# A two-block network on one core: low parts of one weight on GpSimd, rope angles and modulation part 2 in other places

## What is computed

```
mod = c @ w_ada[l] + b_ada[l]
shift_m, scale_m, gate_m, shift_f, scale_f, gate_f = jnp.split(mod, 6, axis=-1)
h = modulate(rms_norm(x, g_pre_mix[l]), shift_m, scale_m)
proj = h @ w_in[l]
q_a, k_a, v_a, q_m, k_m, v_m, o_m, i_m, f_m, g_a, g_m = jnp.split(proj, split_points, axis=-1)
q_a, k_a = rope(q_a, positions), rope(k_a, positions)        # sliding-window attention
qk_m = silu(causal_depthwise_conv(concat([q_m, k_m])))       # mLSTM in chunks of 64
merged = sigmoid(g_a) * (y_a @ w_branch_attn) + sigmoid(g_m) * (y_m @ w_branch_mlstm)
x = x + gate_m * rms_norm(merged @ w_out, g_post_mix)
h2 = modulate(rms_norm(x, g_pre_ffn), shift_f, scale_f)
x = x + gate_f * rms_norm((silu(h2 @ w_gate) * (h2 @ w_up)) @ w_down, g_post_ffn)
```

## Time and profile before

| | |
|---|---|
| median of 3 runs | 820.08 us (815.45 to 822.45) |
| the profiled execution | 822.01 us, of which its span is 820.2 us |
| PE busy | 767.2 us, 94% of the span |
| DVE busy | 638.1 us, 78% |
| ACT busy | 393.8 us, 48% |
| POOL busy | 29.0 us, 4% |
| DMA | 173.67 MB, mean 212 GB/s |

### The profile page before, as it was taken

One profiled execution on the slowest core, in us unless ns is written; L12 is line 12 of the kernel. 1 busy time (PEld: TensorE's weight loads), 2 busy tenths in 40 slices (PEclk: granted clock), 3 DMA queues, 4 the chain that ended last, 5 costly groups with the idle time before them and its releaser, 6 DMA issues.

```text
span 820.2 us, 15828 instructions
## 1 busy us (share of the span) xinstructions
PE 767.2 (94%) x6598; PEld 702.9 (86%) x6598; DVE 638.1 (78%) x838; ACT 393.8 (48%) x554; POOL 29.0 (4%) x44
## 2 busy tenths in 40 slices
PE   0999998998998999999999999989998999999996
PEld 0888998997887999999878987889878999999874
DVE  5759988888986887867987899886599678556457
ACT  3356753575464445344354894533125544454440
POOL 0110000000001000000001000050010000000000
PEclk9999999999999999999999999999999999999999
DMA  9795586682656999989992643600363679565621
GB/s 357 255 343 200 163 258 230 208 281 83 218 188 191 343 318 309 321 279 318 345 348 86 222 147 116 200 3 3 105 226 109 207 243 340 177 196 190 196 97 52
DMA packets 96021, 173.67 MB, mean 212 GB/s; under 512 B 7768, under 2 KB 55231, under 8 KB 95951
## 3 DMA queue, kind: packets, MB, share of 16 engines
q1 hardware_dynamic: 93630, 166.62, 60.9%
q0 software_dynamic: 1872, 5.86, 2.4%
q10 hardware_dynamic: 448, 0.19, 0.1%
HBM read 171.60 MB, written 1.05 MB: 210 GB/s over the span
## 4 chain that ended last, share of the span: by engine, by line
PE 69%; DVE 18%; DMA 6%; ACT 4%; issue 3%; DVEq 0%; POOL 0%; ACTq 0%; POOLq 0%
PE bank L2087 12%; PE bank L2088 12%; PE bank L2089 12%; PE bank L2352 5%; PE bank L2354 4%; PE bank L2353 4%; DVE wlo L459 3%; PE bank L2062 2%; PE bank L2064 2%; PE bank L2063 2%; DMA raw<-in_w_in 2%; DMA cc<-in_c 2%; PE bank L2514 1%; DVE acc L486 1%; DMA raw<-in_w_ada 1%
## 5 line engine op out<-in xcount | busy, mean ns | idle before, releaser
L650 ACT ACTIVATE whi<-raw 128x1024 fp32r<-128x1024 f32 (+1 forms) x212 | 220.9, 1053 | 225.4 <-PE bank L2089 99.2
L459 DVE TENSOR_TENSOR wlo<-raw,whi 128x1024 fp32r<-128x1024 f32 (+1 forms) x212 | 254.2, 1214 | 87.0 <-ACT whi L650 83.3
L2087 PE MATMUL bank<-hh,whi 128*128 128x256 f32 x1016 | 286.3, 282 | 10.7 <-DVE wlo L459 7.4
L2088 PE MATMUL bank<-hl,whi 128*128 128x256 f32 x1016 | 283.8, 279 | 0.0
L2089 PE MATMUL bank<-hh,wlo 128*128 128x256 f32 x1016 | 283.7, 279 | 0.0
L2087 PEld LDWEIGHTS bank<-hh,whi 128*128 128x128 f32 x1016 | 193.1, 190 | 14.8 <-issue 10.2
L2088 PEld LDWEIGHTS bank<-hl,whi 128*128 128x128 f32 x1016 | 192.6, 190 | 0.4 <-issue 0.2
L2089 PEld LDWEIGHTS bank<-hh,wlo 128*128 128x128 f32 x1016 | 192.5, 189 | 0.0
L486 DVE SCALAR_TENSOR_TENSOR acc<-raw,cc,acc 128x1024 f32<-128x1024 f32 x56 | 71.7, 1280 | 5.5 <-DMA raw<-in_w_ada 3.3
L2352 PE MATMUL bank<-whi,ffh 128*128 128x512 f32 x168 | 65.6, 391 | 0.9 <-DVE wlo L459 0.9
L2353 PE MATMUL bank<-wlo,ffh 128*128 128x512 f32 x168 | 65.4, 389 | 0.0
(11 more groups left out here) (453 smaller groups left out, 1081.2 us busy)
## 6 DMA issues: line engine op xcount, KB each, us to landing
raw<-in_w_ada SPq DMA_DIRECT2D x96, 512.0 KB, 5.2
raw<-in_w_in SPq DMA_DIRECT2D x54, 512.0 KB, 4.6
raw<-in_w_ffn_in SPq DMA_DIRECT2D x88, 256.0 KB, 3.9
raw<-in_w_ffn_gate SPq DMA_DIRECT2D x44, 256.0 KB, 4.3
...
```

The source lines that it names most:

```text
L459: eng.tensor_tensor(lo[:, 0:nk * width], raw[:, b % RAW, 0:nk * width], hi[:, 0:nk * width].bitcast(fp), ALU.subtract)\
L650: act.activation(weight_place(g)[0][:, 0:nk * width], raw[:, b % RAW, 0:nk * width], ACT.Copy)\
L2087: mm(o, wh[:, k, c], xh[:, kk_, :], start=first, stop=False)
L2088: mm(o, wh[:, k, c], xl[:, kk_, :], start=False, stop=False)
```

## The change

In the order of the program:

1. The low parts of blocks 2 to 5 of `o_if` are made on POOL, not on DVE. ACT makes the high parts of blocks 4 and 5 between the halves of its scaling, not behind it. POOL does this ahead of its first broadcast loads, and four of these loads now wait until ACT has copied the first half of `qm` (`conv_raw`).
2. PE runs 52 fillers before it turns x, and 40 where it had 32.
3. The angles move behind `km` on DVE, and the biases and `osig` ahead of or into `km`. ACT's sine moves behind its copy of `qm`, ahead of its high parts of `vm`. The small transfers are issued three before each block from number 33 on.
4. Part 2 (`c4`, `c5`) lies beside `km` and `vm`. `kva` and `g1` have nothing beside them; `c6`, `c7`, `c8` lie beside `g2`, `g3`, `ba0`. PE sums part 2 behind `g1`, with 8 fillers in its middle and 8 behind it; the transposes of k that follow wait for DVE to have taken it.

```diff
@@ -110,8 +110,8 @@
-    head = ["c0", "c1", "c2", "c3", "o_if", "qm", "km", "vm", "g0", "qa", "kva", "c8", "g1", "c4", "g2", "c5",
-            "g3", "c6", "ba0", "c7", "ba1", "bm0", "bm1", "wo0", "c9", "wo1"]
+    head = ["c0", "c1", "c2", "c3", "o_if", "qm", "km", "c4", "vm", "c5", "g0", "qa", "kva", "g1", "g2", "c6",
+            "g3", "c7", "ba0", "c8", "ba1", "bm0", "bm1", "wo0", "c9", "wo1"]
     first = [x for j in range(FT // 2) for x in ([f"ff{j}"] + ([f"c{BESIDE_FF[j]}"] if j in BESIDE_FF else []))]
     middle = ["lora", "k", "r", "v", "pv", "pu", "wo2a", "wo3a", "c21", "wo2b", "wo3b"]
@@ -403,7 +403,11 @@
-        ready = [("dve", b + 1) for b in range(len(order))]
+        ready, made_by = [], {"dve": 0, "pool": 0}
+        for o in order:
+            who = "pool" if o[0] == "o_if" and 2 <= o[1] < 6 else "dve"
+            made_by[who] += 1
+            ready.append((who, made_by[who]))
         of_split = {o[6]: b for b, o in enumerate(order) if o[6] is not None}
@@ -421,7 +425,7 @@
         def part_place(d):
-            return {0: (0, 0), 1: (1, 0), 2: (2, 0), 3: (2 * (place["wo0"][0] % 2), 0), 4: (6, 0), 5: (4, 0), 6: (4, 6), 7: (4, 7),
+            return {0: (0, 0), 1: (1, 0), 2: (5, 0), 3: (2 * (place["wo0"][0] % 2), 0), 4: (6, 0), 5: (4, 0), 6: (4, 6), 7: (4, 7),
                     8: (5, 0), 9: (5, 0), 10: (6, 0), 11: (4, 0)}[d]
@@ -529,8 +533,8 @@
                     sp.wait_ge(sem(f"{who}_blocks"), count)
-                if 28 <= b < 37:
-                    for n in (2 * (b - 28), 2 * (b - 28) + 1):
+                if 33 <= b < 39:
+                    for n in range(3 * (b - 33), 3 * (b - 33) + 3):
                         small_transfer(n)
                     sp.dma_start(cut(raw, b % RAW, nk, width)[:, :, a:z], src).then_inc(sem(f"raw{b % RAW}_in"), 16)
@@ -552,6 +556,8 @@
+            prepare_on(pool, "pool", "o_if")
+
@@ -572,6 +578,7 @@
             pool.wait_ge(sem("spreads"), 3 * 16)
+            pool.wait_ge(sem("conv_raw"), 1)
             spread(bcs[:, 1, :], A["sg_ln_g_2"][0], sem("spreads"))
             spread(bc[:, 0, :], A["g_post_mix"][0], sem("spreads"))
@@ -650,7 +657,7 @@
-            def scale_h(u):
+            def scale_h(u, between=None):
                 sh = modT[:, u // 2, (24 if u % 2 else 0):(32 if u % 2 else 8)]
@@ -668,6 +675,8 @@
                            .then_inc(sem("hh_ready"), 1)
+                    if between and half == 0:
+                        between()
@@ -691,8 +700,8 @@
             split("o_if", slice(0, 4))
-            scale_h(0)
-            split("o_if", slice(4, 8))
+            scale_h(0, lambda: split("o_if", slice(4, 6)))
+            split("o_if", slice(6, 8))
             split("qm")
             b0, b1 = item("o_if")
@@ -702,9 +711,6 @@
-
-            act.wait_ge(sem("angles"), 1)
-            act.activation(cossin, rsc[:, 1], ACT.Sin).then_inc(sem("cossin_ready"), 1)
                 for h, b in enumerate(item(name)):
@@ -716,6 +722,8 @@
                 if nxt:
+                    act.wait_ge(sem("angles"), 1)
+                    act.activation(cossin, rsc[:, 1], ACT.Sin).then_inc(sem("cossin_ready"), 1)
                     split(nxt)
             act.wait_ge(sem("if_turned"), 1)
@@ -1194,6 +1202,17 @@
+            dve.wait_ge(sem("osig_ready"), 1)
+            dve.wait_ge(sem("spreads"), 3 * 16)
+            for m in range(MT):
+                TT(st[:, 240 + 8 * m:248 + 8 * m], bank[4 + m][:, 252:260], bsm[:, 0:8], ALU.add)\
+                    .then_inc(sem("if_ready"), 1)
+
+            prepare("km", slice(0, 1))
+            dve.wait_ge(sem(f"pair{place['o_if'][0] % 2}_free"), place["o_if"][0] // 2 + 1)
+            for m in range(MT):
+                step(TT(osig[:, m, :], osig[:, m, :], bcs[:, 0, :], ALU.mult))
+            prepare("km", slice(1, None))
             dve.wait_ge(sem("small_in"), 32)
             step(dve.tensor_copy(st[:, 10:12], posi[:, :]))
@@ -1213,17 +1232,6 @@
-
-            dve.wait_ge(sem("osig_ready"), 1)
-            dve.wait_ge(sem("spreads"), 3 * 16)
-            for m in range(MT):
-                TT(st[:, 240 + 8 * m:248 + 8 * m], bank[4 + m][:, 252:260], bsm[:, 0:8], ALU.add)\
-                    .then_inc(sem("if_ready"), 1)
-
-            dve.wait_ge(sem(f"pair{place['o_if'][0] % 2}_free"), place["o_if"][0] // 2 + 1)
-            for m in range(MT):
-                step(TT(osig[:, m, :], osig[:, m, :], bcs[:, 0, :], ALU.mult))
-            prepare("km")
                 if t == 4:
@@ -1280,7 +1288,8 @@
             prepare("qa", slice(2, 4))
-            prepare("kva", slice(0, 5))
+            prepare("kva")
+            prepare("g1", slice(0, 1))
                 q4 = qr[:, m, :].rearrange("p (i g f c) -> p g i f c", i=4, g=HG, f=2)
@@ -1324,18 +1333,18 @@
             dve.nop().then_inc(sem("arg_ready"), 1)
-            prepare("kva", slice(5, 6))
-            prepare("g1", slice(0, 1))
+            prepare("g1", slice(1, 2))
             dve.wait_ge(sem("cossin_ready"), 1)
             rotate_q(0)
-            prepare("g1", slice(1, 5))
+            prepare("g1", slice(2, 3))
             pair_wait("qa")
             rotate_q(1)
-            prepare("g1", slice(5, 8))
+            prepare("g1", slice(3, 4))
             dve.wait_ge(sem("ka_out"), 2)
                 rotate_k(m)
+            collect_part(2)
             prepare("g2", slice(0, 3))
             for m in range(MT):
@@ -1370,7 +1379,6 @@
             score_max(1, sm1)
-            collect_part(2)
             prepare("g3", slice(0, 1))
             dve.wait_ge(sem("wT_ready"), 8)
@@ -2123,9 +2131,10 @@
             turn_vectors(0, bank[2], n1)
+            run_on(26, 3)
             turn_h(0, lambda m: xn[:, m * D:(m + 1) * D], "xn_ready", 0)
             part(0)
-            run_on(16, 3)
+            run_on(20, 3)
             part(1)
             pe.wait_ge(sem("piece_used"), 1)
@@ -2140,9 +2149,9 @@
             last.then_inc(sem("if_turned"), 1)
+            tokens_out("vm", 512, modulated)
             pe.wait_ge(sem("vectors2_in"), 16 * (len(ROWS2) + 2))
             turn_vectors(1, bank[4], n2)
-            tokens_out("vm", 512, modulated)
             features_out("g0", four, modulated)
@@ -2165,6 +2174,8 @@
             pe.wait_ge(sem("arg_ready"), 1)
+            part(2, lambda: run_on(4, 6))
+            run_on(4, 6)
             pe.wait_ge(sem("qr_ready"), 2)
                 for i in range(4):
@@ -2176,6 +2187,7 @@
             pe.wait_ge(sem("k_scaled"), 1)
+            pe.wait_ge(sem("piece_used"), 3)
             for m in range(MT):
                     last = tr(bank[4 + m][:, h * P:(h + 1) * P], qk[:, 4 + h, m * P:(m + 1) * P], ident)
@@ -2204,7 +2216,6 @@
             pe.wait_ge(sem("s_masked"), 6)
-            part(2)
             for h2 in range(2):
                     for m in range(MT):
@@ -2281,7 +2292,6 @@
-            pe.wait_ge(sem("piece_used"), 3)
             features_out("g3", four, modulated, inside={i: (lambda i=i: between(i)) for i in range(3)})
```

## The result

The changed kernel takes 832.2 us, median of 4 runs (832.0 to 834.2), where before took 819.4 us on the same chip (815.5 to 822.5). The ratio is 1.016 [1.012, 1.020]. It is slower by 1.6%; the prediction said no change, with 827 us as its upper end. In a second measurement on another chip it took 831.2 against 823.4 us, ratio 1.013 [1.009, 1.018]. The profiled execution took 832.25 us, its span is 830.4 us: 10.2 us more than before. Single profiles of a kernel scatter, so the medians, 12.8 us apart, and these spans need not agree.

What follows compares the result with a forecast made beforehand. PE's queue was taken to bound the kernel, busy for 767.2 of 820.2 us. The terms summed to +1.15 us; from the median, 820.1 + 1.1 gave 821 us, with a range of 814 to 827 us.

Steps and rivals of the forecast that it cites:

- The wait at km: PE's 3.05 us wait before `km` and the slow clock behind it go, as the angles move: -4.85 us.
- The wait at vm: DVE's list makes `vm` start at 73.1 us where PE is ready at 69.2: a new wait of +3.9 us.
- The one us that I had added for `km`'s fourth block: One us added to DVE's way to `vm`, because that block's transfer is issued late, behind four small ones.
- The slow clock: PE at half clock in 3.4 us stretches, costing about 1.7 us each; a new one behind the `vm` wait, +1.7 us.
- whether the clock falls behind them again is even odds: The slow stretch at 113.6 us, behind small matmuls around `kva`, counted as half gone: -0.8 us.
- The start: Up to PE's first real matmul: fillers and POOL's low parts gain 0.7 to 1.9 us, taken as -1.7 us.
- qa: DVE's lead over PE in `qa` falls from three blocks to one: +1.2 us.
- g0: DVE's low parts alternate with convolution tiles, 3.15 us each against PE's 2.75: +1.1 us, part of it taken as hidden.
- g1: Nothing stands beside `kva` and `g1` any more, so the wait of 0.9 us in `g1` goes: -0.9 us.
- Part 2's own price: Part 2's small matmuls and 16 fillers push the scores, less covered waits and DVE time returned: +1.5 us in all.
- Late loads: Rival: blocks of `km` and `c4` land 4 us later, each late us being PE's wait at `vm`: 825 us, chance 8%.
- The clock does not last: Rival: PE cools between the early fillers and the transposes; the start costs 1.0 us instead of gaining 1.7: 824 us, chance 24%.

Runs made afterwards that it cites:

- POOL undone: The changed kernel with all low parts of `o_if` back on DVE and ACT's copies in their old order; 828.8 us, ratio 1.008 to the kernel before.
- fillers undone: The changed kernel without the 52 fillers ahead of the transposes and with 32, not 40, before part 1; 826.6 us, ratio 1.006 to the kernel before.

## Why the prediction was wrong, point by point

**The wait at km.** The size, -4.85 us, was measured as -4.9. The cause was not as I put it. The clause "since the low part of `km`'s first block no longer stands behind the angles" describes the edit, but the wait also goes with the angles left where they were: the step that failed is the one that I did not price, POOL's wait for `conv_raw`, which lets `qm`'s third block land in 3.9 us and not in 9.5. A consequence I missed: the change had no need to move the angles.

**The wait at vm: the step that failed most.** The forecast was "so DVE goes on at 47.9, and ACT's high part of `km` (1.1 us) holds it to 49.2 us", with 22.9 us of list behind it. Measured, DVE's first low part of `km` starts at 53.22 us, 4.0 us later, since ACT's high part waits for PE's first block of `qm`. Of the 4.0 some 2.4 are PE's own delay (`qm` at 49.12 and not 46.7), which moves the end of the wait too and so costs nothing. Most of the other 1.6 is the ring that I had left out: with PE as forecast, `qm`'s first block ends at 49.45, and a low part cannot begin before 50.6. The list then took 24.6 us, 1.7 more than forecast. The four tiles were right, 8.0 and 8.04, but my 4.8 for angles, biases and `osig` met 4.84 for the angles alone, of which 1.6 are the cast held up beside POOL, and 1.4 for `osig`. The one us that I had added for `km`'s fourth block was not needed: ACT waited for PE there, not for the transfer. Together 1.6 + 1.7 - 1.0 us, and 0.3 in small gaps and roundings, on top of 3.9 make the 6.5 us. I had summed an engine's work as though it could run ahead, while a ring of four slots ties it to PE.

**The slow clock.** The sum gave every slow stretch the length of those before, 3.4 us, and 1.7 us of cost. Here they were 3.4 (`o_if`), 10.2 (the wait and `vm`), and 6.8 us (small matmuls and `kva`), and `vm` alone grew by 2.8 us, from 11.1 to 13.9. A stretch in `o_if` was not in the sum at all, though the sum had PE standing there until DVE was done. The clause "whether the clock falls behind them again is even odds" was a saving of 0.8 us that became a loss of 1.6 in this profile and neither loss nor gain in the second one. A slow stretch in `kva` is there in every profile but two (POOL undone, fillers undone).

**The start.** Gain 0.8 us, at the lower end of the 0.7 to 1.9 that I had given, where the sum had taken 1.7: POOL met DVE twice. The Trainium skill, page SBUF — State Buffer, section "Who interferes with whom", names `tensor_scalar` and `cast` too among the operations that can take the pair of ports shared with GpSimd, and says that the other side then blocks fully; the trace agrees, with 1.22 against 0.17 us for the TENSOR_SCALAR at L1153, and 1.75 against 0.17 us for the cast.

**qa, g0, g1, part 2.** +1.2 at `qa` was right. `g0`'s waits did not show, because the slow clock in `vm` hid them; with `vm` at full clock one of 1.85 us appeared. `g1` gained 1.6 instead of 0.9. Part 2's own price, +1.5, was measured at +1.5, by some luck in its parts: +1.8 ahead of the scores (forecast 2.2), -1.7 where the small matmuls had stood behind `g2`, and +1.4 about `g3`, where PE waits 1.25 and 1.53 us and before has one wait of 1.17.

**The rivals.** "Late loads" had the right sign for the wrong reason: ACT's high parts of `km` all waited for PE, none for a load. "The clock does not last" occurred in full in one of two profiles and cost half a microsecond at `o_if`, not 2.7. The chance of 6% for slower by over 1% was too low: it hung on late loads and the start's clock, and what came were a longer wait at `vm` and slow stretches of up to 10.2 us, which no rival had.

What stays open: why the slow stretch at a wait of 5 to 9 us is 6.8 us long in some profiles and 10.2 in others; what the 2.2 us behind `ff0` are; and how much of the loss each part bears, which the intervals (0.3% each) don't separate.
